# Fewer small matmuls between the products of a three-layer kernel: additions on GpSimd, stacked cumulative sums, a rotation on VectorE, and a last norm in another order

## The reference, cut to what matters

```python
# layer 1: retention, 8 heads of 128; q and k are rotated first
cos, sin = jnp.cos(ang), jnp.sin(ang)
rotary = jnp.concatenate([t1 * cos - t2 * sin, t1 * sin + t2 * cos], axis=-1)   # t1, t2: halves of a head
# layer 2: SSD, 32 heads in 4 groups, chunks of 128
a_cum = jnp.cumsum((dt * a)..., axis=2)
decay = jnp.exp(jnp.where(causal, a_cum[:, :, :, None] - a_cum[:, :, None, :], -jnp.inf))
y_b = y_b * silu(ssd_z)                                 # (tokens, 4 groups, 512)
y_b = y_b * lax.rsqrt(jnp.mean(y_b * y_b, axis=-1, keepdims=True) + EPS)
# layer 2 also: memory attention, 4 heads (softmax over 256 keys), and a gated short convolution
# ahead of every layer, and at the end
rms_norm_2 = x * lax.rsqrt(jnp.mean(x * x, axis=-1, keepdims=True) + EPS) * w
# layer 3: rope(positions) on MLA queries and keys
```

## Time and profile before

| what | value |
|---|---|
| median of 3 runs | 1805.3 us (1802.9 to 1808.76) |
| the profiled execution | 1803.28 us, span of its instructions 1801.5 us |
| TensorE (PE) busy | 1750.1 us, 97% of the span |
| VectorE busy | 1290.0 us, 72% |
| ScalarE busy | 899.0 us, 50% |
| GpSimd busy | 120.3 us, 7% |
| granted TensorE clock, mean | 0.991 of full speed |
| summing matmuls L1818 | 70 records, 35 matmuls |
| spread matmuls L2001 | 64 |
| GpSimd additions L581, L583 | 15 of 128x512 (26.1 us), 15 of 128x256 (17.2 us) |

### The profile page before, as it was taken

How to read it: one execution, slowest core, us unless ns; L and a number is a source line. 1 busy time by engine, 2 the same in 40 slices (tenths; PEclk the granted TensorE clock), 3 DMA queues, 4 the chain that set the end, 5 groups by cost and what they waited for, 6 DMA issues and landing times.

```text
span 1801.5 us, 24340 instructions
## 1 busy us (share of the span) xinstructions
PE 1750.1 (97%) x9667; PEld 1498.1 (83%) x9667; DVE 1290.0 (72%) x1634; ACT 899.0 (50%) x1158; POOL 120.3 (7%) x147
## 2 busy tenths in 40 slices
PE   5899999999999999999999999999999999999997
PEld 4788888777888888888888888788888888888885
DVE  6888978785677756888677676975554667778654
ACT  4444443444456445665344666644444545566531
POOL 2411101000010100001000000000000000000000
PEclk9999999999999999999999999999999999999998
DMA  9989979774555566666555555566566565444562
GB/s 324 361 310 331 345 225 324 234 251 134 149 152 164 187 176 187 186 180 184 164 142 142 158 156 167 164 191 188 183 189 180 157 202 144 140 129 129 175 187 94
DMA packets 311889, 350.70 MB, mean 195 GB/s; under 512 B 11248, under 2 KB 286832, under 8 KB 311776
## 3 DMA queue, kind: packets, MB, share of 16 engines
q1 hardware_dynamic: 297792, 298.34, 55.1%
q0 software_dynamic: 13984, 50.80, 8.0%
HBM read 347.00 MB, written 2.10 MB: 194 GB/s over the span
## 4 chain that ended last, share of the span: by engine, by line
PE 73%; DVE 15%; ACT 6%; issue 3%; DMA 2%; POOL 0%; SPq 0%; ACTq 0%; DVEq 0%
PE psG L484 40%; PE psG L485 20%; DVE w_lo L418 4%; ACT w_hi L414 3%; PE psG L478 2%; PE psG L480 2%; PE psG L479 2%; PE psH L1818 1%; DMA raw<-in_mem_w 1%; DVE P L1186 1%; DVE P L1181 1%; PE psH L1832 1%; PE psH L1807 1%; DMA raw<-in_w_in 0%; DVE P L1501 0%
## 5 line engine op out<-in xcount | busy, mean ns | idle before, releaser
L484 PE MATMUL psG<-xA,w_hi 128*128 128x512 f32 x2624 | 948.6, 405 | 3.1 <-DVE w_lo L418 2.5
L418 DVE TENSOR_TENSOR w_lo<-raw,w_hi 128x1024 fp32r<-128x1024 f32 (+1 forms) x560 | 690.0, 1243 | 252.4 <-ACT w_hi L414 251.0
L485 PE MATMUL psG<-xA,w_lo 128*128 128x256 f32 x2624 | 736.5, 281 | 0.0
L414 ACT ACTIVATE w_hi<-raw 128x1024 fp32r<-128x1024 f32 (+1 forms) x560 | 569.4, 1043 | 233.1 <-PE psG L485 167.8
L484 PEld LDWEIGHTS psG<-xA,w_hi 128*128 128x128 f32 x2624 | 493.7, 188 | 126.0 <-issue 8.8
L485 PEld LDWEIGHTS psG<-xA,w_lo 128*128 128x128 f32 x2624 | 496.4, 189 | 4.2 <-issue 3.4
L484 PE MATMUL psG<-yP,w_hi 128*128 128x512 f32 x960 | 338.5, 396 | 3.5 <-DVE P L1186 1.6
L485 PE MATMUL psG<-yP,w_lo 128*128 128x256 f32 x960 | 269.2, 280 | 0.0
L484 PEld LDWEIGHTS psG<-yP,w_hi 128*128 128x128 f32 x960 | 179.9, 187 | 46.3 <-DVE P L1186 1.9
L453 ACT ACTIVATE P<-psG 128x512 f32<-128x512 f32 (+2 forms) x103 | 60.9, 592 | 251.0 <-PE psG L485 251.0
L485 PEld LDWEIGHTS psG<-yP,w_lo 128*128 128x128 f32 x960 | 181.4, 189 | 0.2
(11 more groups left out here) (318 smaller groups left out, 1761.5 us busy)
## 6 DMA issues: line engine op xcount, KB each, us to landing
raw<-in_w_in SPq DMA_DIRECT2D x360, 512.0 KB, 3.8
raw<-in_w_out SPq DMA_DIRECT2D x128, 512.0 KB, 3.5
ada_ring<-in_w_ada POOLq DMA_DIRECT2D x96, 512.0 KB, 6.3
raw<-in_mem_w SPq DMA_DIRECT2D x32, 512.0 KB, 8.8
raw<-in_w_uq SPq DMA_DIRECT2D x24, 384.0 KB, 3.3
raw<-in_w_ukv SPq DMA_DIRECT2D x32, 128.0 KB, 2.5
raw<-in_w_ukv SPq DMA_DIRECT2D x16, 256.0 KB, 3.4
P<-in_memT SPq DMA_DIRECT2D x4, 512.0 KB, 5.8
```

The costliest lines, as they stand in the source:

```text
L414: nc.scalar.activation(high(n), low(n, raw), ACT.Copy).then_inc(hi_ready, 1)
L418: nc.vector.tensor_tensor(low(n), low(n, raw), high(n), ALU.subtract).then_inc(lo_ready, 1)
L484: nc.tensor.matmul(psG[:, bank + f, :], hi[:, w], x, start=first, stop=False)
L485: last = nc.tensor.matmul(psG[:, bank + f, S:2 * S], lo[:, w], x[:, 0:S], start=False, stop=end)
```

## The change

It does five things. (1) The rotation of q and k in `rt_hook` is no longer a matmul: VectorE multiplies each half of a head by the sine while writing it to the other half of the partitions (two instructions on 64 partitions, at p = 0); the sine of the upper half is negated once. ScalarE's decay exponentials no longer wait for the rotation. (2) The high and low parts of the cumulative sums stand one above the other (`cum_hl`, 64 rows), so that one matmul with K = 64 spreads both. (3) In `yb_hook` GpSimd adds the four squared tiles to one (two additions for each group), and TensorE sums with one matmul; nearly all positions move: ScalarE 0, 4, 8, 10 to 2, 6, 9, 13, VectorE 2, 6, 13 to 4, 8, 15, TensorE 9 to 12. `mem_hook` keeps its positions. In `sc_hook` ScalarE moves 0, 2, 8 to 2, 3, 9, and VectorE 2, 4, 6, 10 to 4, 6, 7, 11. (4) For norms 2 and 3 GpSimd also adds group 3 (one matmul in place of four); TensorE sums at p = 9 in place of 7 and ScalarE takes the root at p = 11 in place of 9. (5) In the last norm the gain is applied ahead of time by ScalarE (`gained_4`, 16 copies of 128 x 256, twelve of them during the product), group 2 is summed inside the product, group 3 in two parts (tiles 12 and 13 squared and added before the product ends; 14 and 15 squared behind it and summed by two matmuls), and the scaling by the root is three VectorE multiplications of 128 x 1024 and one on GpSimd, stored in the order 1, 2, 0, 3.

The diff, cut to its core:

```diff
-        cum_hi = sb("cum_hi", [NP, S], F32R, place=in_p(CUM + 1))
-        cum_lo = sb("cum_lo", [NP, S], F32R)
+        cum_hl = sb("cum_hl", [NP, S], F32R, place=in_p(CUM + 1))
+        cum_hi, cum_lo = cum_hl[0:SSD_HEADS, :], cum_hl[SSD_HEADS:2 * SSD_HEADS, :]
...
-            for g in range(4):
-                sp.wait_ge(q["fin_y"], 4 * g + 4)
+            for g in (1, 2, 0, 3):
+                sp.wait_ge(*((q["fin_y"], g) if g else (q["fin_pool"], 1)))
...
             def add_squares(n):
-                for g in range(3):
+                for g in range(4 if n in (2, 3) else 3):
...
+            for g in range(4):
+                a = W[:, 1024:2048]
+                pool.wait_ge(q["yb_sq"], g + 1)
+                nc.gpsimd.tensor_tensor(a[:, 0:512], a[:, 0:512], a[:, 512:1024], ALU.add).then_inc(q["yb_pre"], 1)
+                pool.wait_ge(q["yb_pre"], 2 * g + 1)
+                nc.gpsimd.tensor_tensor(a[:, 0:S], a[:, 0:S], a[:, S:512], ALU.add).then_inc(q["yb_pre"], 1)
...
             add_squares(4)
+            a = norm_squares(4, 3)
+            pool.wait_ge(q["nm_sq"], 20)
+            nc.gpsimd.tensor_tensor(a[:, 0:S], a[:, 0:S], a[:, S:512], ALU.add).then_inc(q["nm_pre"], 1)
+            pool.wait_ge(q["nm_rs"], 6)
+            pool.wait_ge(q["gained"], 16)
+            y = P[:, 0:4, :]
+            nc.gpsimd.tensor_tensor(y, y, norm_root_of(4).unsqueeze(1).broadcast_to([NP, 4, S]), ALU.mult).then_inc(q["fin_pool"], 1)
...
-                    if b == 0 and p == 9:
+                    if b == 0 and p == 11:
                         norm_inverse_root(n)
...
 (ScalarE, yb_hook)
-                if p == 0:
+                if p == 2:
                     log_part(W[:, 0:1024], tiles(SSZ + 4 * g, 4)).then_inc(q["gate_log"], 1)
-                if p == 4:
+                if p == 6:
                     sigmoid(W[:, 0:1024], "yb", g + 1)
-                if p == 8:
+                if p == 9:
                     act.wait_ge(q["yb_y"], g + 1)
                     f(W[:, 1024:2048], tiles(XS + 4 * g, 4), ACT.Square).then_inc(q["yb_sq"], 1)
-                if p == 10:
+                if p == 13:
                     act.wait_ge(q["yb_ss"], g + 1)
...
 (ScalarE, last norm)
+            def gained_4(t):
+                f(P[:, t, :], xT[:, t, :], ACT.Copy, scale=V("final_norm", t)).then_inc(q["gained"], 1)
...
+            f(norm_squares(4, 3)[:, 512:1024].rearrange("p (t s) -> p t s", t=2), xT[:, 14:16, :], ACT.Square).then_inc(q["nm_sq"], 1)
+            gained_4(14)
+            gained_4(15)
             norm_inverse_root(4)
...
 (VectorE, rt_hook)
+                if p == 0:
+                    landed(dve, G_RTQK)
+                    v.tensor_tensor(turned[low], q_and_k[up, :, 2 * n:2 * n + 2, :], sin4[up], ALU.mult)
+                    v.tensor_tensor(turned[up], q_and_k[low, :, 2 * n:2 * n + 2, :], sin4[low], ALU.mult).then_inc(q["rt_s"], 1)
                 if p == 3:
-                    dve.wait_ge(q["rt_rot"], n + 1)
-                    v.tensor_tensor(heads(rt_qk[:, 0:512], 2), heads(psH[:, BA, :], 2), sin2, ALU.mult)
-                    v.tensor_tensor(heads(rt_qk[:, 512:1024], 2), heads(psH[:, BB, :], 2), sin2, ALU.mult)\
-                     .then_inc(q["rt_s"], 1)
...
 (VectorE, yb_hook)
-                if p == 6:
+                if p == 8:
                     dve.wait_ge(q["gate_sig"], GATE["yb"] + g + 1)
                     link(v.tensor_tensor(W[:, 0:1024], tiles(SSZ + 4 * g, 4), W[:, 0:1024], ALU.mult))
                     v.tensor_tensor(y, y, W[:, 0:1024], ALU.mult).then_inc(q["yb_y"], 1)
...
 (VectorE, the end)
             dve.wait_ge(q["nm_rs"], 6)
-            for t in range(KT):
-                v.scalar_tensor_tensor(out=P[:, t, :], in0=xT[:, t, :], scalar=V("final_norm", t), in1=norm_root_of(4),
-                                       op0=ALU.mult, op1=ALU.mult).then_inc(q["fin_y"], 1)
+            dve.wait_ge(q["gained"], 16)
+            for g in range(1, 4):
+                y = P[:, 4 * g:4 * g + 4, :]
+                v.tensor_tensor(y, y, norm_root_of(4).unsqueeze(1).broadcast_to([NP, 4, S]), ALU.mult).then_inc(q["fin_y"], 1)
...
 (TensorE)
-                if p == 0:
-                    if n:
-                        pe.wait_ge(q["rt_y"], n)
-                    mm(psH[:, BA, :], C1("rot128"), tiles(RTQ + 2 * n, 2), start=True, stop=True)
-                    mm(psH[:, BB, :], C1("rot128"), tiles(RTK + 2 * n, 2), start=True, stop=True)\
-                        .then_inc(q["rt_rot"], 1)
...
-                    if b == 0 and p == 7:
+                    if b == 0 and p == 9:
                         sum_squares(n, (2, 3))
...
-                            for part in (cum_hi, cum_lo):
-                                ins = mm(psH[:, BB + j // 2, (j % 2) * S:(j % 2) * S + S], head,
-                                         part[0:SSD_HEADS, :], start=part is cum_hi and j % 2 == 0,
-                                         stop=part is cum_lo and j % 2 == 1)
+                            ins = mm(psH[:, BB + j // 2, (j % 2) * S:(j % 2) * S + S], head,
+                                     cum_hl[0:2 * SSD_HEADS, :], start=j % 2 == 0, stop=j % 2 == 1)
...
-                if p == 9:
-                    pe.wait_ge(q["yb_sq"], g + 1)
-                    for j in range(4):
-                        ins = mm(psH[:, BA, 0:S], ones, W[:, 1024 + j * S:1024 + j * S + S], start=j == 0, stop=j == 3)
-                    ins.then_inc(q["yb_ss"], 1)
+                if p == 12:
+                    pe.wait_ge(q["yb_pre"], 2 * g + 2)
+                    mm(psH[:, BA, 0:S], ones, W[:, 1024:1024 + S], start=True, stop=True).then_inc(q["yb_ss"], 1)
...
+                if b == 3 and p == 14:
+                    sum_squares(4, [2])
             run_products(pe, G_OUT1, out1_hook)
-            sum_squares(4, (2, 3))
+            pe.wait_ge(q["nm_pre"], 18)
+            a = norm_squares(4, 3)
+            mm(psH[:, norm_bank(4), 0:S], ones, a[:, 0:S], start=False, stop=False)
+            pe.wait_ge(q["nm_sq"], 21)
+            mm(psH[:, norm_bank(4), 0:S], ones, a[:, 512:512 + S], start=False, stop=False)
+            mm(psH[:, norm_bank(4), 0:S], ones, a[:, 512 + S:1024], start=False, stop=True).then_inc(q["nm_ss"], 1)
```

More of the change, by code:

```diff
@@ L796, in rt_hook @@
                 if p == 3:
-                    act.wait_ge(q["rt_rot"], n + 1)
+                    if n:
+                        act.wait_ge(q["rt_y"], n)
                     for h in range(2):
@@ L864, in dt_hook @@
                     act.wait_ge(q["dt_cum"], 1)
-                    f(ident_r[0:SSD_HEADS, :], ident[0:SSD_HEADS, 0:SSD_HEADS], ACT.Copy)
-                    f(cum_hi[0:SSD_HEADS, :], P[0:SSD_HEADS, CUM, :], ACT.Copy).then_inc(q["cum_hi"], 1)
+                    for rows_of in (slice(0, SSD_HEADS), slice(SSD_HEADS, 2 * SSD_HEADS)):
+                        f(ident_r[rows_of, :], ident[rows_of, rows_of], ACT.Copy)
+                    f(cum_hi, P[0:SSD_HEADS, CUM, :], ACT.Copy).then_inc(q["cum_hi"], 1)
             def conv_hook(v, p):
@@ L969, in sc_hook @@
                           scale=V("sc_w", 3 * t + 2)).then_inc(q["sc_tap"], 1)
[L970 removed]
+                if p == 3:
                     log_part(W[:, 1024:2048], tiles(SCZ + 4 * v, 4)).then_inc(q["gate_log"], 1)
[L972 removed]
+                if p == 9:
                     sigmoid(W[:, 1024:2048], "sc", v + 1)
@@ L1087, in _ @@
             squares_4 = square_hook(4, G_OUT1)
+            def gained_4(t):
+                f(P[:, t, :], xT[:, t, :], ACT.Copy, scale=V("final_norm", t)).then_inc(q["gained"], 1)
             def out1_hook(b, p):
                 squares_4(b, p)
+                if b == 1 and p == 6:
+                    act.wait_ge(q["f3_lo"], 4)
+                if b and p in (8, 9):
+                    for t in range(4 * b - 4 + 2 * (p - 8), 4 * b - 2 + 2 * (p - 8)):
+                        gained_4(t)
+                if b == 3 and p == 16:
+                    landed(act, G_OUT1, 7)
+                    act.wait_ge(q["nm_ss"], 18)
+                    f(norm_squares(4, 3)[:, 0:512].rearrange("p (t s) -> p t s", t=2), xT[:, 12:14, :], ACT.Square).then_inc(q["nm_sq"], 1)
+                    gained_4(12)
+                    gained_4(13)
                 if b:
@@ L1331, in _ @@
             gate_columns(1)
-            sin2 = C1("sin", S).unsqueeze(1).broadcast_to([NP, 2, S])
+            up_sin = con1[64:128, CON1["sin"]:CON1["sin"] + S]
+            link(v.tensor_scalar(up_sin, up_sin, -1.0, None, ALU.mult))
+            sin4 = C1("sin", S).unsqueeze(1).unsqueeze(1).broadcast_to([NP, 2, 2, S])
+            q_and_k = tiles(RTQ, 16).rearrange("p (a t s) -> p a t s", a=2, t=8)
+            turned = rt_qk.rearrange("p (a t s) -> p a t s", a=2, t=2)
+            low, up = slice(0, 64), slice(64, 128)
             def rt_hook(n, p):
+                if p == 0:
+                    landed(dve, G_RTQK)
```

(21 more changed lines are left out.)

31 lines of the change are left out of this document (12 added, 19 removed).

## The result

The changed kernel takes 1817.35 us (median of 20 runs, 1807.7 to 1824.2), the kernel before 1803.61 (20 runs, 1795.2 to 1808.8): ratio 1.0069, 95% interval 1.0057 to 1.0081. It is slower by 0.7%. The profiled execution took 1817.96, its span 1816.1 against 1801.5 before.

What follows compares the result with a forecast made beforehand. TensorE, busy 97% of the span, bounds the kernel. Terms -4.7 + 0 + 10.3 - 1.3 + 3.2 - 1.0 - 0.5 = +6.0 us on 1803.3 give 1809.3, 1811.3 as a median; own range 1806 to 1816, wider 1796 to 1820.

Steps and rivals of the forecast that it cites:

- the rival in which GpSimd also holds up the division: Group norm: GpSimd's additions also exclude VectorE's two multiplications by a column, 7.9 us more in all, 1819.2; chance 0.18.
- Group norm: Four stretches: TensorE waits 2.3 us at the transposes for VectorE's division and its clock falls; 10.3 us longer in all.
- Rotation: Four stretches without the rotation matmuls: 1.7, 1.55, 0.7 and 0.7 us saved, 4.7 off in all.
- Stacked sums: Eight SSD hooks: TensorE comes 0.94 us earlier and waits 0.94 longer at p = 13; counted 0.
- Norm 2: Six matmuls fewer, nothing urgent behind them: 1.3 us off.
- Norm 3: Positions load issued late, TensorE waits 3.0 us at chunk 4, 1.5 added for the clock: 3.2 us longer.
- Short convolution: Old waits at chunks 4 and 11 end; waits of 1.9 and 2.7 us appear; 1.0 us off taken.
- The end: Last norm: root 2.45 us earlier, group 2's sum costs 0.43, VectorE and GpSimd exclude each other, stores bunch: 0.5 off.
- TensorE's busy time: Whole kernel: expected to go down by some 18 us at full clock.
- The forecast's sum without its falls: Rival that the clock stays up behind the waits: five times 1.5 us off the sum, 1.5 off in all, 1803.8; chance 0.20.

Runs made afterwards that it cites:

- kernel 2: The changed kernel without GpSimd's additions in the group norm, new positions kept, four summing matmuls at p = 12: 1820.2 us, ratio 1.0084 to the kernel before.
- kernel 1: The changed kernel with the group norm's stretches put back as they were before: 1802.6 us, ratio 0.9999 to the kernel before.
- kernel 3: The changed kernel with the memory head's division ahead of the gate multiplications on VectorE, the one sum at p = 13: 1797.8 us, ratio 0.9971.
- kernel 5: The changed kernel with the SSD's stacked sums undone, eight matmuls of 32 rows in each hook: 1819.9 us, ratio 1.0072 to the kernel before.
- kernel 7: The changed kernel with the last scaling of all four groups on VectorE, stores in the order 0 to 3: 1812.7 us, ratio 1.0042.
- kernel 10: The changed kernel with only the short convolution's positions put back as before: 1817.2 us, ratio 1.0088 to the kernel before.
- kernel 4: The changed kernel with GpSimd issuing the positions and mask loads ahead of the addition of norm 3's last group: 1814.2 us, ratio 1.0056.
- kernel 11: The changed kernel with early group norm gates, GpSimd's additions, one sum at p = 11, positions' load first and last scaling on VectorE: 1801.1 us, ratio 0.9989.
- any mended form of the whole: The changed kernel with positions' load first, last scaling on VectorE, and either the memory head's division first (1796.4 us) or the group norm as before (1794.5 us).

## Why the prediction was right

The direction and the mechanism held: TensorE waits at the transposes for VectorE's division, and its clock falls behind that wait. The size did not. The time came out 6.0 us above the 1811.3 given, outside the text's own range (1806 to 1816) and inside the wider one (1796 to 1820). Nearest to it is the rival in which GpSimd also holds up the division (1819.2, given 0.18), and its mechanism is what the trace shows. As a difference the forecast fares worse: +6.0 was said and +13.7 measured. The level of 1811.3 stood on a median of three runs of the kernel before, 1805.3, which came to 1803.6 in twenty. By its own steps:

- **Group norm: right in kind, mis-sized.** The order of VectorE's queue gives the wait forecast (2.2 us in kernel 2, 2.3 said, and without a fall a stretch 2.3 longer with its four sums, where 1.07 and 1.3 were said), and the clock falls behind it (1.5 to 1.8 us each in kernel 2, 1.5 said). What was missing from the sum is what the text had as a rival, GpSimd holding up the division: no more than one of its two additions, 1.5 us for each stretch instead of 1.98. The term was 10.3 and measures 16.3. By the Trainium skill (SBUF — State Buffer, Who interferes with whom), weighed in that rival, tensor_scalar can take the lock as well; kernels 2 and after agree, 0.62 us alone and 2.14 beside the addition. I gave the rival 0.18 where the page was right.
- **Rotation: right**, each stretch to 0.15 us in the run that isolates it, 4.4 in the four against 4.7 (5.0 with the 0.6 behind them).
- **Stacked sums: right**, 0, the matmuls turned into waiting.
- **Norm 2: right** as far as it can be told: 6.8 less 5.0 leaves 1.8, 1.3 said; no run has it alone.
- **Norm 3: the wait right** (2.71 against 3.0), the clock's fall not there in the profile after, so 1.7 against 3.2. That one profile is mild. Counted from TensorE's products ahead of the sum to the next copy of a block, the six other profiles with this order (kernels 1, 2, 3, 5, 7 and 10) all have the fall. Kernels 7 and 10, with loads of 3.3 and 3.5 us (3.3 said), are 3.2 longer than before, as forecast; the four with loads of 3.8 to 4.8 are 3.7 to 5.4 longer. What the step lacked is the scatter of the load.
- **Short convolution: the waits right** (1.71 and 2.38 against 1.9 and 2.7), the gain 2.3 where 1.7 was said for a clock that stays up. With the fall, in kernels 4, 5 and 11, it is 0.7 to 1.0, where 0.2 was said; the forecast took 1.0.
- **The end: right in kind, in part by luck.** The root came 2.3 earlier with group 2's sum counted in (2.0 said). The two engines did exclude each other: together they took 5.64 us, where 6.0 was said for one behind the other, and three stores were issued from 4.5 on (4.8 said). The stores landed 1.1 later behind the scaling's start (1.5 said), but 0.9 more passed behind the last landing, which no step had.
- **TensorE's busy time** went down by 11 us, not by 18; the 18 were counted at full clock, and matmuls take longer where the clock is low.

At full clock, as under 1, the kernels come to 1785.3 before and 1787.6 after: of the 13.7 us between the medians some 2.3 are matmuls and waits, and the rest goes with a mean clock of 0.985 in place of 0.991. The forecast's sum without its falls was -1.5; with GpSimd's part of the stretches (4.07 less a fall of 1.65 is 2.42, 1.35 above the 1.07 said, four times: +5.4) and the better rotation and convolution (-0.3 and -1.3) it would have been +2.3. In kernels 7 and 10 one stretch each had the wait of 3.7 with its clock up, and was 2.6 and 2.8 longer; priced by these it would have been +3.4. That the start was 6.8 us longer in the profile after is nothing the change did: other profiles with the same code there lie on both sides of the kernel before.

What stays open: why the clock falls behind one wait and not behind another of the same length, and with it a share of the falls in the twenty runs that one profile can't place. The stages of the profile after, less its start, make 7.8 us; norm 3, at 1.7 in that profile and 3.2 to 5.4 in six others, may be a part of what is missing to 13.7.

## What to carry to other kernels

Before a matmul is taken out of a full TensorE, look at which engine's queue ends just as TensorE meets it: here the transposes and the SSD's products were met to 0.1 to 0.3 us, so that a saving ahead of them could only become waiting, and work put in front of the division on VectorE cost twice, by its length and by the clock behind it. Work moved to GpSimd is not free for VectorE, so it belongs where VectorE is idle or reads PSUM. A late hand-off through a DMA brings the DMA's own scatter into the time: issue it ahead of queued arithmetic. And try the parts of a change one by one: the rotation alone gave as much by the medians as any mended form of the whole.

## What the runs showed of the hardware

The clock's fall doesn't hang on the length of the wait ahead of it alone. In all twelve profiles of the changed kernels and the one of before, it fell behind 6 of the 11 waits of TensorE from 1.95 to 2.24 us that stand between 700 and 1400 us (the four of kernel 11 without a fall), behind 5 of the 10 last waits of the short convolution of 2.3 to 2.4 us, behind 2 of the 3 of 2.7 us, behind all 4 from 3.2 to 4.2 us in norm 3, and behind 18 of the 20 of 3.7 us in the group norm. Behind none of the 13 waits from 1.57 to 1.71 us did it fall. The stretch behind the second wait of kernel 11, 2.09 us long, with the clock up; 2.08 us brought it down in the kernel before:

```profile
1050.00:1053.00 3.00, 3.00 (x20) 2.63 (x18) 0.77 (x1) 0.75 (x3) 0.00 (x0) 1.00 0.04 6
```

One of the two exceptions among the waits of 3.7 us is the third of kernel 7:

```profile
1079.00:1082.00 3.00, 3.00 (x17) 2.61 (x17) 1.23 (x1) 1.26 (x3) 0.00 (x0) 1.00 0.35 78
```

So such a fall is better priced by a chance than as certain: in about half of the cases behind waits of 2 to 3 us. It cost 1.5 to 1.8 us in kernel 2; by the two exceptions against the same stretches of the kernel after (2.6 and 2.8 longer for 3.9 and 4.1) it cost 1.3 to 1.4. In four stretches (two of kernel 5, one each of kernels 7 and 10) the low clock lasted longer (0.52 on average from 1023 to 1030 us in kernel 10), and they were 4.8 to 5.2 us longer than before instead of some 4.
